# Rounded-part products in the convolution block's first projection, and a fifth depthwise block on TensorE

## The reference, cut to what matters

```python
def conformer_conv(h, w_in, b_in, dw_w, dw_b, ln_g, ln_b, w_out, b_out):
    val, gate = jnp.split(h @ w_in + b_in, 2, axis=-1)      # 1024 -> 2 x 1024
    u = val * jax.nn.sigmoid(gate)
    u = depthwise_conv_centred(u, dw_w) + dw_b              # 31 taps along the tokens
    u = jax.nn.silu(layer_norm(u, ln_g, ln_b))
    return u @ w_out + b_out
```

## Time and profile before

| | us |
|---|---|
| three executions | 1334.14, 1335.85, 1338.22 (median 1335.85) |
| the profiled execution | 1335.61, of which the span is 1333.8 |
| TensorE busy in the span | 1259.6 (94%) |
| VectorE busy | 897.2 (67%) |
| ScalarE busy | 532.5 (40%) |
| GpSimd busy | 124.3 (9%) |

### The profile page before, as it was taken

How to read it: one execution, slowest core, us unless ns; L and a number is a source line. 1 busy time by engine, 2 the same in 40 slices (tenths; PEclk the granted TensorE clock), 3 DMA queues, 4 the chain that set the end, 5 groups by cost and what they waited for, 6 DMA issues and landing times. The chain is left out here.

```text
span 1333.8 us, 19412 instructions
## 1 busy us (share of the span) xinstructions
PE 1259.6 (94%) x7350; PEld 992.9 (74%) x7350; DVE 897.2 (67%) x1540; ACT 532.5 (40%) x892; POOL 124.3 (9%) x165
## 2 busy tenths in 40 slices
PE   4999979989999998999999999899999999899997
PEld 1777645555888887885588888777878988788886
DVE  0547886444777776695777777489977645777776
ACT  2664266323444444014544444311226543544443
POOL 0061012000000001100000000245530000000000
PEclk8999989999999998999999999899999999999999
DMA  9312377984655542330465555124323333555551
GB/s 390 143 71 95 137 292 280 389 315 143 239 187 186 186 169 72 130 124 6 184 231 187 186 187 189 64 109 145 139 101 137 142 111 126 176 187 185 187 185 57
DMA packets 24950, 225.80 MB, mean 169 GB/s; under 512 B 2737, under 2 KB 2865, under 8 KB 4658
## 3 DMA queue, kind: packets, MB, share of 16 engines
q1 hardware_dynamic: 23328, 220.31, 45.2%
q10 hardware_dynamic: 1554, 4.56, 1.0%
HBM read 223.81 MB, written 1.05 MB: 169 GB/s over the span
## 5 line engine op out<-in xcount | busy, mean ns | idle before, releaser
L945 PE MATMUL psum<-aT_r,arena_r 128*128 128x512 f32 x920 | 327.5, 398 | 1.6 <-DVE arena_r L2312 1.1
L2312 DVE TENSOR_TENSOR arena_r<-ring,arena_r 128x1024 fp32r<-128x1024 f32 x188 | 220.2, 1220 | 99.6 <-ACT arena_r L1685 99.6
L946 PE MATMUL psum<-aT_r,arena_r 128*128 128x256 f32 x920 | 258.1, 280 | 0.0
L1685 ACT ACTIVATE arena_r<-ring 128x1024 fp32r<-128x1024 f32 x188 | 186.8, 1051 | 143.7 <-PE psum L980 133.2
L980 PE MATMUL psum<-arena_r 128*128 128x512 f32 x876 | 213.4, 392 | 0.0
L824 PE MATMUL psum<-aT,ring 128*128 128x256 f32 (+1 forms) x896 | 210.7, 394 | 0.0
L945 PEld LDWEIGHTS psum<-aT_r,arena_r 128*128 128x128 f32 x920 | 172.8, 188 | 44.0 <-issue 2.2
L824 PEld LDWEIGHTS psum<-aT,ring 128*128 128x128 f32 x896 | 170.1, 191 | 38.8 <-issue 17.5
L980 PEld LDWEIGHTS psum<-arena_r 128*128 128x128 f32 x876 | 159.5, 188 | 34.7
L946 PEld LDWEIGHTS psum<-aT_r,arena_r 128*128 128x128 f32 x920 | 173.6, 189 | 2.6
L1697 ACT ACTIVATE nrm<-nrm 128x256 f32<-128x256 f32 x76 | 31.8, 418 | 165.9 <-DVE nrm L2330 162.7
(11 more groups left out here) (535 smaller groups left out, 1846.0 us busy)
## 6 DMA issues: line engine op xcount, KB each, us to landing
ring<-in_w_ffn SPq DMA_DIRECT2D x44, 1536.0 KB, 6.8
ring<-in_w_mod SPq DMA_DIRECT2D x32, 1536.0 KB, 8.7
ring<-in_w_ff SPq DMA_DIRECT2D x32, 1024.0 KB, 4.8
ring<-in_w_in_g SPq DMA_DIRECT2D x8, 1536.0 KB, 6.3
ring<-in_w_conf_i SPq DMA_DIRECT2D x8, 1024.0 KB, 4.9
ring<-in_w_hyb_f SPq DMA_DIRECT2D x4, 1536.0 KB, 6.8
ring<-in_w_in_a SPq DMA_DIRECT2D x4, 1536.0 KB, 6.5
ring<-in_w_in_b SPq DMA_DIRECT2D x4, 1536.0 KB, 6.4
```

The lines of the kernel that those rows point to most:

```text
L945: mm(bank(use).rearrange("p (a t) -> p a t", a=2), hi, x_both[:, :, k, :], start=(k == 0), stop=False)
L946: last = mm(bank(use)[:, T:2 * T], lo, x_hi[:, k, :], start=False, stop=(k == KT - 1))
L1685: fn(out_hi[2] if last_out else w_hi[j % 2][:, at], slot(c)[:, at], ACT.Copy).then_inc(split_hi, 1)
L2312: tt(lo, slot(c)[:, at], hi.bitcast(F32), ALU.subtract).then_inc(split_ready, 1)
```

## The change

Chunks 1 to 7 of the first projection are made of rounded parts as in the gates. ACT rounds the input (four instructions) and the 14 half chunks of weights; DVE makes the 4 low parts of the input and the 14 of the weights, in place in the ring. TensorE makes three products of 256 columns for each of the 16 float32 products of a chunk. Chunk 0 stays as it is. Block 3 moves from DVE to TensorE, so DVE has blocks 0 and 1 as a group and block 2 alone, and POOL builds a fifth set of tap matrices ahead of `margins`. DVE's later `glu_in` steps come at every third step of the convolution, with the split of a chunk two further on ahead of each. DVE's low parts of the input stand in its program behind the wait for `margins`.

```diff
-CONV_PE = (4, 5, 6, 7)
+CONV_PE = (3, 4, 5, 6, 7)
...
+        def conf_weights(c, half, t=None):
+            return out_weights(FIRST["conf_i"] + c, half, t), conf_hi[2 * (c % 3) + half]
...
-        taps = [x[:, at:at + D] for x in (yT_t, ybuf_t) for at in (0, D)]
+        taps = [x[:, at:at + D] for x in (yT_t, ybuf_t) for at in (0, D)] + [o_t[:, 0:D]]
+        conf_x, conf_x_hi, conf_x_lo = aT[:, :, 0:T], view(aT_r, 0, KT, 2 * T)[:, :, T:2 * T], view(arena_r, 7168, KT, T)
+        conf_hi = [arena_r[:, at:at + D] for at in (9216, 10240, 11264)] + [x[:, 0:D] for x in (z_r, rowbc_r, decay_r)]
...
-                feature_block(use, slot(c0 + c)[:, 0:D], lambda k: aT[:, k, 0:T], fresh=() if c else (3,))
-                filled(feature_block(use, slot(c0 + c)[:, D:2 * D], lambda k: aT[:, k, 0:T], T), use)
+                if c == 0:
+                    feature_block(use, slot(c0 + c)[:, 0:D], lambda k: aT[:, k, 0:T], fresh=(3,))
+                    filled(feature_block(use, slot(c0 + c)[:, D:2 * D], lambda k: aT[:, k, 0:T], T), use)
+                    return
+                pe.wait_ge(conf_x_split, 4)
+                for half in range(2):
+                    pe.wait_ge(conf_w_lo, 2 * (c - 1) + half + 1)
+                    w_lo_c, w_hi_c = conf_weights(c, half, ring_r)
+                    out_cols = bank(use)[:, half * T:half * T + T]
+                    for k in range(KT):
+                        at = slice(k * P, k * P + P)
+                        mm(out_cols, w_hi_c[:, at], conf_x_hi[:, k, :], start=(k == 0), stop=False)
+                        mm(out_cols, w_lo_c[:, at], conf_x_hi[:, k, :], start=False, stop=False)
+                        last = mm(out_cols, w_hi_c[:, at], conf_x_lo[:, k, :], start=False, stop=(k == KT - 1))
+                filled(last, use)
...
+            for kp in range(4):
+                pair = slice(2 * kp, 2 * kp + 2)
+                wait_read(act, USE["norm3"][kp])
+                fn(conf_x_hi[:, pair, :], conf_x[:, pair, :], ACT.Copy).then_inc(conf_x_rounded, 1)
+
+            def conf_round(c):
+
+                n = FIRST["conf_i"] + c
+                act.wait_ge(ring_ready[SLOT_OF[n]], 16 * (TURN_OF[n] + 1))
+                for half in range(2):
+                    raw, rounded = conf_weights(c, half)
+                    fn(rounded, raw, ACT.Copy).then_inc(conf_w_hi, 1)
+
+            conf_round(1)
...
             for c in range(7):
                 glu_gate(c)
+                if c == 0:
+                    conf_round(2)
+                if 3 + c < KT:
+                    conf_round(3 + c)
...
+            def conf_split(c):
+
+                for half in range(2):
+                    dve.wait_ge(conf_w_hi, 2 * (c - 1) + half + 1)
+                    (raw, rounded), (low, _) = conf_weights(c, half), conf_weights(c, half, ring_r)
+                    tt(low, raw, rounded.bitcast(F32), ALU.subtract).then_inc(conf_w_lo, 1)
+
+            for kp in range(4):
+                pair = slice(2 * kp, 2 * kp + 2)
+                dve.wait_ge(conf_x_rounded, kp + 1)
+                tt(conf_x_lo[:, pair, :], conf_x[:, pair, :], conf_x_hi[:, pair, :].bitcast(F32),
+                   ALU.subtract).then_inc(conf_x_split, 1)
+            conf_split(1)
             own = [c for c in range(KT) if c not in CONV_PE]
             ahead = iter(range(2, KT))
             glu_in(0)
+            conf_split(2)
+            conf_split(3)
             glu_in(1)
...
-                    if k % 7 == 0:
+                    if k % 3 == 0:
 
                         for c in ahead:
+                            if c + 2 < KT:
+                                conf_split(c + 2)
                             glu_in(c)
                             break
```

More of the change, by code:

```diff
@@ L612, in build @@
         csig_ready, conv31, csq_ready, csq_done = sem("csig_ready"), sem("conv31"), sem("csq_ready"), sem("csq_done")
+        conf_x_rounded, conf_x_split = sem("conf_x_rounded"), sem("conf_x_split")
+        conf_w_hi, conf_w_lo = sem("conf_w_hi"), sem("conf_w_lo")
         ln_sd, ln_x, conf_out = sem("ln_sd"), sem("ln_x"), sem("conf_out")
```

## The result

The changed kernel takes 1338.62 us (median of 20 executions, 1335.75 to 1342.05), the kernel before 1333.45 us (median of 20, 1331.36 to 1338.22): 5.2 us more, ratio 1.0037 with a 95% interval of 1.0028 to 1.0045. It is slower, and the cause is at the place that the prediction named. The profiled execution has a span of 1337.9 us, 4.1 us more than before; its convolution stage alone is 6.1 us longer.

A forecast was written before the change was run, and what follows sets the result against it. TensorE was taken to bound the convolution stage, VectorE 3.7 us ahead of it. Stall +5.7, clock +1.5, products -8.4 and block +5.6 gave +4.4 us on the profiled 1335.61: 1340.0 us, range 1337.0 to 1343.0.

The forecast's parts named there:

- the place that the prediction named: Start of chunk 1: TensorE waits for DVE's low parts, queued behind the wait for `margins`; a 5.7 us stall.
- The stall: Before chunk 1: `margins` at 539.2 us holds DVE's low parts, so TensorE starts at 543.0 us, 5.7 us lost.
- The clock: TensorE in chunk 1, after the stall: products at 1.2 GHz for a stretch, costing 1.5 us (bounds 0 and 2.9).
- Products: Chunks 1 to 7 on TensorE: rounded products every 0.119 us, 5.71 us a chunk instead of 6.91, saving 8.4 us.
- The block: One more convolution block on TensorE, taps 3.70 us and sum 1.87 us, all on the path: +5.57 us.
- The tie: End of the convolution: DVE's last step (616.2 us) and TensorE's seventh norm sum (616.3 us) meet within 0.1 us.
- The sum of the stage: TensorE up to the norm's sums: stall, clock, products and block together +4.4 us, sums starting at 613.3 us.
- the first (clock back sooner): Rival at chunk 1: low clock falls on the stall, less than 1.1 us lost; +2.9 to +4.0 us; chance 0.22.
- The second (VectorE as the bound): Rival at the convolution's end: DVE's tail 2 us longer, so the last sum waits; +6.4 us, 1342.0; chance 0.10.
- The third: Rival in chunks 1 to 7: products at 0.109 us each; +1.0 to +2.0 us, 1337; chance 0.05.
- The fourth, no stall: Rival before chunk 1: DVE gets `margins` during chunk 0; -2.8 us, 1332.8; chance 0.05 including any other gain.
- The sentence on the port: DVE two-input and GpSimd SBUF instructions exclude each other; without the wait, part of the gain would be lost again.

The follow-up runs named there:

- filler: Changed kernel, with TensorE making 13 unneeded float32 products while it waits before chunk 1; ratio 1.0023 to the kernel before.
- taps_late: Changed kernel, GpSimd raising `margins` first and building tap matrices only after VectorE's low parts of chunk 1's weights; ratio 0.9984 to the kernel before.
- margins_first: Changed kernel, with GpSimd clearing its margins and raising the semaphore ahead of the five tap matrices; ratio 1.0038 to the kernel before.

## Why the prediction was right

1340.0 us was forecast from the profiled execution, +4.4 us; measured are +5.2 us between the medians, with 1338.62 us inside the range of 1337.0 to 1343.0. The median of before had itself moved from 1335.85 us (three executions) to 1333.45 us (20), so the difference is the better test: right in sign, 0.8 us too small. Step by step:

- **The stall.** Right. `margins` was to come 9.96 us after chunk 0's start (539.2 less 529.24); it came 9.94 us after (536.94 less 527.00). The first split was to end 13.7 us after it and ended after 13.6 (540.61). The idle stretch was 6.6 us instead of 5.7 only because chunk 0 took 7.0 us instead of 8.1: its clock had already risen, and GpSimd's work doesn't get faster with TensorE's. The two differences cancel. (The written sum is 0.1 us too high: 539.2 + 2.4 + 1.2 are 542.8, not 542.9. Nothing hangs on it.)
- **The clock.** The mechanism was right, the size was off: this is the term that was mis-sized. 1.5 us were taken and 2.9 was the upper bound. Chunk 1 took 8.5 us (540.75 to 549.21) against 5.76, so 2.7 us; `filler` got 2.6 us back. A row behind an idle stretch of 4 us had been taken for one of 6.6 us, and the low level lasted 3.4 us in the one and 10.3 in the other, 4.3 of it during the idle stretch and 5.9 in chunk 1. The other row was the better sign: behind 4.3 us of idle time the low level lasted 6.8 us, up to 531.3. But no row gives the size for certain: before chunk 0 the changed kernel has the same idle stretch of 4.32 us, and there the low level lasted 3.4 us.
- **Products.** 0.120 us in all seven chunks rather than 0.119, 5.76 us a chunk: 8.0 us saved for 8.4.
- **The block.** 5.57 us, to the hundredth (587.75 to 593.32).
- **The tie.** Right: VectorE's end (615.67) and TensorE's seventh sum (612.62 + 3.02 = 615.64) are 0.03 us apart.
- **The sum of the stage.** -1.1 (chunk 0's clock) + 6.8 (chunk 1 due at 534.0, started at 540.75) + 2.7 - 8.0 + 5.6 + 0.1 (last sum) = +6.1 us, measured 6.07. The forecast of +4.4 us had the clock's cost 1.2 us too small and the products' saving 0.4 us too large, so for these two executions it was 1.7 us too small. It came nearer to the medians, which lie 5.2 us apart; what makes up the 0.9 us between that and 6.1 isn't shown by one profile of each kernel, and this nearness is in part luck. One cause of such differences is visible: in the kernel before, chunk 0 costs what its clock makes of it (8.1 us in this profile), while in the changed kernel chunk 1 starts 13.7 to 13.8 us after chunk 0 at either speed.

Of the rivals, the first (clock back sooner) didn't come about in the profile: the low stretch began in the stall but lasted far into chunk 1. The second (VectorE as the bound) isn't the case, but is 0.03 us away. The third is refuted by 0.120 us a product. The 109 ns behind it came from the formula of the Trainium skill ("TensorE: Matmul & The Clock Gate", "Back-to-back issue gap"), which that section gives for an isolated matmul only. For a stream with a weight load ahead of each matmul, as here, it has 81 ns at 128 columns and 131 ns at 512, and the 120 ns measured at 256 lie between the two; the formula should not have been used for a chunk. The fourth, no stall, was priced at -2.8 us (-2.4 with 8.0 for the products), and `taps_late` is it: -2.3 us of stage. But the condition given there was wrong. It said that it would do if VectorE got `margins` early, with part of the gain lost on the port; in `margins_first` all of it is lost. The sentence on the port had the mechanism, from one meeting, and didn't work out four in a row: 4 x 2.26 us are 9.0 us, as much as the wait (6.54 us) and the low parts behind it (2.42 us) together.

## What to carry to other kernels

When a change puts new work behind an old wait, look at what the wait stood behind: it was free only because nobody needed what followed it. Removing the wait alone isn't enough if the two engines then meet on a shared resource; what has to move is the work that isn't urgent (here tap matrices that are needed 40 us later). And two halves of a change, each slower alone (1.0033 and 1.0139), can be faster together (0.9984), though here only once the order of the third engine was right: without that they are 1.0037.

## What the runs showed of the hardware

- VectorE's two-input operations and GpSimd's products alternated where both had work queued: 2.26 us for a pair of 128x512 on VectorE (0.62 us alone) and 128x992 on GpSimd (1.85 us alone), four times in a row. Side by side cost nearly as much as one after the other.
- An idle stretch of 6.6 us on TensorE brought a low clock of about 10 us and cost 2.6 to 2.7 us on top. The same wait filled with 5.6 us of unneeded products kept the clock at 1.00. The length of the low stretch doesn't follow from the idle time alone: behind idle stretches of 4.32 us it was 6.8 us in the kernel before and 3.4 us in the changed one.
- At 1.2 GHz a rounded product of 256 columns starts every 0.21 us, at 2.4 GHz every 0.120 us, with no difference between the seven chunks, whose weights lie in four buffers.
